# Two per-head totals as split fp32r matmuls, the request-state reads moved to the opening of a pair, and a reordered start, in a hybrid RWKV-7 decoder layer

## The reference

```python
n = rmsnorm(x, norm1)
c_rw, c_att, c_gate = _split(n @ w_in, (RW_COLS, ATT_COLS, GATE_COLS))
# RWKV-7 branch, 16 heads of 64
kk = heads(k * k_k)
kk = kk * lax.rsqrt(jnp.maximum(jnp.sum(kk * kk, axis=-1, keepdims=True), 1e-24))   # squared keys, total per head
S = S * w_t + sa[..., None] * b_t + v_t[..., None] * k_t                            # state, token by token
y = (y - mean) * lax.rsqrt(var + GN_EPS) * lnx_w + lnx_b                            # mean and variance per head
bonus = jnp.sum(r_h * k_h * r_k, axis=-1, keepdims=True) * v_h                      # total per head
out = (y + bonus) * g
# sparse attention branch, then
h = x + (sig(g_rw) * (o_rw @ p_rw) + sig(g_att) * (o_att @ p_att)) @ w_o
h = h + conv_glu(rmsnorm(h, norm2))
```

## Time and profile before

| | us |
|---|---|
| median of 3 runs | 1778.01 |
| range of the runs | 1776.01 to 1780.81 |
| profiled execution | 1776.88 |
| its span | 1775.3 |

### The profile page before, as it was taken

One profiled execution on the slowest core, in us unless ns is written; L12 is line 12 of the kernel. 1 busy time (PEld: TensorE's weight loads), 2 busy tenths in 40 slices (PEclk: granted clock), 3 DMA queues, 4 the chain that ended last, 5 costly groups with the idle time before them and its releaser, 6 DMA issues.

```text
span 1775.3 us, 40657 instructions
## 1 busy us (share of the span) xinstructions
PE 1758.8 (99%) x16482; PEld 1708.2 (96%) x16482; DVE 1120.7 (63%) x2015; ACT 759.6 (43%) x1059; POOL 53.8 (3%) x103
## 2 busy tenths in 40 slices
PE   9999999999999999999999999999999999999997
PEld 9999899999999998999999999999999999999997
DVE  7764864667777777665566666666666665444443
ACT  6456444555555554333443333333333333333332
POOL 2500000000000000000000000000000000000000
PEclk9999999999999999999999999999999999999998
DMA  7644344433333332644454444444444444555553
GB/s 285 220 165 165 124 162 157 143 115 118 112 112 117 112 111 103 220 166 170 171 220 163 157 164 158 168 161 167 164 165 165 165 165 167 172 169 175 170 169 134
DMA packets 51697, 283.47 MB, mean 160 GB/s; under 512 B 7248, under 2 KB 11856, under 8 KB 25776
## 3 DMA queue, kind: packets, MB, share of 16 engines
q1 hardware_dynamic: 43488, 260.32, 41.9%
q10 hardware_dynamic: 3888, 12.59, 1.9%
q0 software_dynamic: 4256, 9.65, 1.8%
HBM read 274.26 MB, written 8.27 MB: 159 GB/s over the span
## 4 chain that ended last, share of the span: by engine, by line
PE 96%; DVE 3%; DMA 0%; ACT 0%; issue 0%; DVEq 0%; ACTq 0%
PE bank L621 30%; PE bank L623 28%; PE bank L622 28%; PE bank L945 1%; PE bank L985 1%; DVE w_lo L567 1%; DVE scores L1939 1%; PE bank L642 0%; PE bank L643 0%; PE bank L644 0%; DMA w_raw<-in_w_in 0%; PE bank L905 0%; DVE max L1906 0%; PE bank L852 0%; PE bank L800 0%; PE bank L817 0%
## 5 line engine op out<-in xcount | busy, mean ns | idle before, releaser
L621 PE MATMUL bank<-x_split,w_lo 128*128 128x288 f32 x2880 | 872.8, 303 | 2.8 <-DVE w_lo L567 2.1
L622 PE MATMUL bank<-x_split,w_hi 128*128 128x288 f32 x2880 | 849.6, 295 | 0.0
L623 PE MATMUL bank<-x_split,w_hi 128*128 128x288 f32 x2880 | 847.2, 294 | 0.0
L587 ACT ACTIVATE w_hi<-w_raw 128x2048 fp32r<-128x2048 f32 (+1 forms) x262 | 468.7, 1789 | 591.8 <-PE bank L623 579.1
L567 DVE TENSOR_TENSOR w_lo<-w_raw,w_hi 128x2048 fp32r<-128x2048 f32 (+1 forms) x238 | 503.8, 2117 | 283.2 <-ACT w_hi L587 282.9
L621 PEld LDWEIGHTS bank<-x_split,w_lo 128*128 128x128 f32 x2880 | 540.3, 188 | 18.0 <-issue 8.2
L622 PEld LDWEIGHTS bank<-x_split,w_hi 128*128 128x128 f32 x2880 | 541.0, 188 | 2.6 <-issue 1.5
L623 PEld LDWEIGHTS bank<-x_split,w_hi 128*128 128x128 f32 x2880 | 542.2, 188 | 0.0
L621 PE MATMUL bank<-act_split,w_lo 128*128 128x288 f32 x704 | 208.5, 296 | 0.0
L622 PE MATMUL bank<-act_split,w_hi 128*128 128x288 f32 x704 | 207.7, 295 | 0.0
L623 PE MATMUL bank<-act_split,w_hi 128*128 128x288 f32 x704 | 207.0, 294 | 0.0
(11 more groups left out here) (396 smaller groups left out, 1544.2 us busy)
## 6 DMA issues: line engine op xcount, KB each, us to landing
w_raw<-in_w_up SPq DMA_DIRECT2D x88, 1024.0 KB, 4.8
w_raw<-in_w_in SPq DMA_DIRECT2D x47, 1024.0 KB, 4.9
w_raw<-in_w_down SPq DMA_DIRECT2D x64, 704.0 KB, 4.1
w_raw<-in_w_gate SPq DMA_DIRECT2D x32, 1024.0 KB, 4.8
w_raw<-in_w_p SPq DMA_DIRECT2D x16, 1024.0 KB, 4.9
w_raw<-in_w_o SPq DMA_DIRECT2D x16, 1024.0 KB, 4.8
h<-in_x ACTq DMA_DIRECT2D x1, 2304.0 KB, 11.2
h_spill<-h ACTq DMA_DIRECT2D x1, 2304.0 KB, 9.3
```

Source lines behind the costliest of these rows:

```text
L587: actv(WHI[:, slot, 0:kt], WRAW[:, slot, 0:kt], ACT.Copy).then_inc(sem("w_hi"), 3 if isinstance(n, int) and n == 2 else 1)
L621: mm(out, wl, hi, start=first and k == ks[0], stop=False, skip_group_check=True)
L622: mm(out, w, lo, start=False, stop=False, skip_group_check=True)
L623: ins = mm(out, w, hi, start=False, stop=last and k == ks[-1], skip_group_check=True)
```

## The change

- `kk_sum` and `bonus_mm` take their operand in rounded part and remainder (`SQS`, `RKS`, fp32r) and a matrix of ones in fp32r (`HONES`), in two matmuls each. ACT squares the keys twice (fp32 and rounded), DVE subtracts (`kk_lo`); for the bonus DVE copies `RKR` into its rounded part and subtracts, each waiting for the one before. Mean and variance stay as they are.
- The 16 products with `SIN` go from behind the fourth inverse step to a pair's opening, between lines 912 and 916. The wait for `bonus` comes with them, and the transposed columns move within bank 4.
- The chunk map of the last chunk has its own tile `MT3`; DVE makes five additions for the maps in place of four.
- DVE's additions to `SIN` (`s_grown`) come ahead of the last chunk's state, not behind it.
- In the first quarter of the first unit the x tiles 0 and 1 are rounded ahead of the weights, and PE starts with the four products that need rounded weights alone.

The start, on PE, ACT and DVE:

```diff
+                        if s == 0 and u == 0:
+                            pe.wait_ge(sem("w_part_hi"), 1)
+                            for k in range(2):
+                                pe.wait_ge(sem("x_split"), k + 1)
+                                mm(out, WHI[:, 0, k], XN[:, 0, k], start=k == 0, stop=False, skip_group_check=True)
+                                mm(out, WHI[:, 0, k], XN[:, 1, k], start=False, stop=False, skip_group_check=True)
...
+                        if s == 0 and u == 0:
+                            for k in range(2):
+                                mm(out, WLO[:, 0, k], XN[:, 0, k], start=False, stop=False, skip_group_check=True)
-                        for k in range(4):
+                        for k in range(2 if s == 0 and u == 0 else 0, 4):
...
+            first_hi(0, 2, "x_in0")
             act.wait_ge(sem("w_first_in"), 16)
             first_weights(0, [0])
-            first_hi(0, 2, "x_in0")
...
+            dve.wait_ge(sem("norms_in"), 16)
+            first_lo(0, 2)
             first_weights(0, [0])
-            dve.wait_ge(sem("norms_in"), 16)
-            first_lo(0, 4)
+            first_lo(2, 4)
```

The totals, on PE, ACT and DVE:

```diff
+            def head_sum(bank, split):
+                mm(BK[bank][:, 0:N], HONES[:], split[:, 1, :], start=True, stop=False, skip_group_check=True)
+                return mm(BK[bank][:, 0:N], HONES[:], split[:, 0, :], start=False, stop=True, skip_group_check=True)
             def kk_sum(v):
-                pe.wait_ge(sem("kk_sq"), v)
-                mm(BK[3][:, 0:N], head_ones, SQK[:], start=True, stop=True).then_inc(sem("kk_sum"), 1)
+                pe.wait_ge(sem("kk_sq"), 2 * v)
+                head_sum(3, SQS).then_inc(sem("kk_sum"), 1)
...
-                mm(BK[4][:, 0:N], head_ones, RKR[:], start=True, stop=True).then_inc(sem("bonus_mm"), 1)
+                head_sum(4, RKS).then_inc(sem("bonus_mm"), 1)
...
-                actv(SQK[:], RKV[:, 1, :], ACT.Square, scale=PRM[:, PR_KK:PR_KK + 1]).then_inc(sem("kk_sq"), 1)
+                for dst in (SQK[:], SQS[:, 0, :]):
+                    ins = actv(dst, RKV[:, 1, :], ACT.Square, scale=PRM[:, PR_KK:PR_KK + 1])
+                ins.then_inc(sem("kk_sq"), 1)
...
+            def kk_lo(v):
+                dve.wait_ge(sem("kk_sq"), 2 * v - 1)
+                V.tensor_tensor(SQS[:, 1, :], SQK[:], SQS[:, 0, :].bitcast(F32), ALU.subtract).then_inc(sem("kk_sq"), 1)
...
-                V.scalar_tensor_tensor(RKR[:], RKV[:, 0, :], PRM[:, PR_RK:PR_RK + 1], KP[:], ALU.mult,
-                                       ALU.mult).then_inc(sem("rkr"), 1)
+                st.done(V.scalar_tensor_tensor(RKR[:], RKV[:, 0, :], PRM[:, PR_RK:PR_RK + 1], KP[:], ALU.mult, ALU.mult))
+                st.done(V.tensor_copy(RKS[:, 0, :], RKR[:]))
+                V.tensor_tensor(RKS[:, 1, :], RKR[:], RKS[:, 0, :].bitcast(F32), ALU.subtract).then_inc(sem("rkr"), 1)
...
+            st.done(V.tensor_copy(HONES[:], head_ones))
+            kk_lo(1)
             streamed(FILL_FIRST)
             kk_max(1)
```

The pair, on PE (between lines 912 and 916; the same products go at 971 to 975, the wait for `bonus` at 924) and on DVE (the additions to `SIN` go from behind the loop over the chunks into its last pass):

```diff
+                pe.wait_ge(sem("bonus"), v)
+                pe.wait_ge(sem("sin_in"), v * 16)
+                settle(pe)
+                for r in range(2):
+                    for g, q in enumerate(quads):
+                        for e, h in enumerate(halves):
+                            mm(BK[(4, 7)[e]][q, 256 + r * HD:256 + (r + 1) * HD], ARS[h, r].rearrange("p x n -> p (x n)"), SIN[h, 4 * r + g, :],
+                               start=True, stop=True)
...
-                    ins = grown(grow, 0, 1, MTB[h, 2, e * HD:(e + 1) * HD], ST[h, 2, :], e, 1)
+                    ins = grown(grow, 0, 1, MT3[h], ST[h, 2, :], e, 1)
...
+                    if c == 3:
+                        dve.wait_ge(sem("state_s_mm"), v)
...
                     dve.wait_ge(sem("state_mm"), v * 3 - 3 + c)
                     state(c)
...
+                if not last:
+                    kk_lo(it + 2)
                 dve.wait_ge(sem("y_mm"), v)
```

More of the change, by code:

```diff
@@ L191 @@
 ATT_STEPS = [("sample", 0), (0, 0), (0, 1), (1, 0), (1, 1), ("sample", 1)]
-PAIR_STEPS = 16
+PAIR_STEPS = 18
 TOKEN_TILES = (0, P, N - P)
@@ L390, in build @@
     LO = m("l_off", [P, 2, 2 * BL])
-    MTB = m("chunk_map", [P, NCH - 1, P])
+    HONES = m("head_ones_r", [P, P], F32R)
+    MTB = m("chunk_map", [P, NCH - 2, P])
+    MT3 = m("chunk_map_3", [P, CH])
     MLS = region(vv_at)("m_low_s", [NS, 2, NS])
@@ L398, in build @@
     RKR = m("r_k_rk", [P, N])
+    RKS = m("r_k_rk_split", [P, 2, N], F32R)
+    assert m.at <= inv_at + 3 * size_of([P, 4, CH])
+    SQS = region(r0)("squares_k_split", [P, 2, N], F32R)
     m = region(big)
@@ L631, in first_units @@
                     for u in range(FIRST):
+                        out = BK[first_bank(u)][:, 0:N]
+                        if s == 0 and u == 0:
[4 more added lines that the diff above has]
+                                mm(out, WHI[:, 0, k], XN[:, 1, k], start=False, stop=False, skip_group_check=True)
                         if s < 2 and u < 3:
@@ L635, in first_units @@
                             pe.wait_ge(sem("w_split"), s + 1)
-                        out = BK[first_bank(u)][:, 0:N]
-                        for k in range(4):
+                        if s == 0 and u == 0:
+                            for k in range(2):
+                                mm(out, WLO[:, 0, k], XN[:, 0, k], start=False, stop=False, skip_group_check=True)
+                        for k in range(2 if s == 0 and u == 0 else 0, 4):
                             t = 4 * s + k
@@ L912, in pair @@
                             mm(BK[5 + e][q, tt * P:tt * P + BL], BT[h, c0:c0 + BL], AR[h, 0, c0:c0 + BL], start=True, stop=True)
+                quads = [slice(g * BL, (g + 1) * BL) for g in range(4)]
+                pe.wait_ge(sem("bonus"), v)
[6 more added lines that the diff above has]
+                               start=True, stop=True)
                 for tt, par in chunks:
@@ L923, in pair @@
                 ins.then_inc(sem("b_mm"), 1)
-                pe.wait_ge(sem("bonus"), v)
-                settle(pe)
                 for tt, par in chunks:
@@ L935, in pair @@
                 settle(pe)
-                tr(BK[4][:, 288:416], BKV[:].rearrange("p x n -> p (x n)"), ident).then_inc(sem("k_mm"), 1)
+                tr(BK[4][:, 384:512], BKV[:].rearrange("p x n -> p (x n)"), ident).then_inc(sem("k_mm"), 1)
                 fill(5)
-                quads = [slice(g * BL, (g + 1) * BL) for g in range(4)]
                 def blockwise(bank, lhs, rhs, both=False):
@@ L964, in pair @@
                 blockwise(3, L2, T)
-                pe.wait_ge(sem("sin_in"), v * 16)
                 pe.wait_ge(sem("mats"), v)
@@ L970, in pair @@
                 ins.then_inc(sem("l2s_mm"), 1)
[L971 to L975, removed]
                 for tt in range(2):
@@ L1512, in pair @@
                 for rows in (slice(0, 2 * NS), slice(2 * NS, P)):
-                    actv(TOKS[rows, 0, :], BK[4][0:2 * NS, 288:416], ACT.Copy)
-                actv(TOKS[NS:2 * NS, 1, :], BK[4][P - NS:P, 288:416], ACT.Copy).then_inc(sem("toks_sb"), 1)
+                    actv(TOKS[rows, 0, :], BK[4][0:2 * NS, 384:512], ACT.Copy)
+                actv(TOKS[NS:2 * NS, 1, :], BK[4][P - NS:P, 384:512], ACT.Copy).then_inc(sem("toks_sb"), 1)
                 if not last:
@@ L2230, in pair @@
                 state(0)
[L2231 to L2236, removed]
+                for c, src in ((1, BK[7][:, P:P + CH]), (2, BK[6][:, P + CH:2 * P])):
+                    for e, h in enumerate(halves):
+                        V.tensor_tensor(MTB[h, c - 1, e * HD:(e + 1) * HD], src[h], eye_ch[h], ALU.add)
+                V.tensor_tensor(MT3[:], BK[7][:, P + CH:2 * P], eye_ch, ALU.add).then_inc(sem("map"), 1)
                 rv = AR[:, 1, :].rearrange("p (c f) -> p c f", f=CH)
@@ L2247, in pair @@
                         mix_prev(it + 1, 0)
+                    if c == 3:
+                        dve.wait_ge(sem("state_s_mm"), v)
+                        for r in range(2):
+                            half = SIN[:, 4 * r:4 * r + 4, :]
+                            ins = V.tensor_tensor(half, half, BK[(5, 2)[r]][:, 0:256].rearrange("p (b f) -> p b f", f=HD), ALU.add)
+                        ins.then_inc(sem("s_grown"), 1)
                     dve.wait_ge(sem("state_mm"), v * 3 - 3 + c)
                     state(c)
[L2250 to L2254, removed]
+                if not last:
+                    kk_lo(it + 2)
                 dve.wait_ge(sem("y_mm"), v)
```

## The result

| | before | after |
|---|---|---|
| median of the runs, us | 1776.39 (20 runs) | 1780.88 (20 runs) |
| range of the runs, us | 1774.76 to 1780.81 | 1779.27 to 1783.40 |
| profiled execution, us | 1776.88 | 1781.10 |
| its span, us | 1775.3 | 1779.5 |

After to before: 1.0022, 95% interval 1.0016 to 1.0029. The changed kernel is 4.5 us slower, less than the 0.3% that the prediction set as its bound for a difference. It forecast +4.4 us. (The 1778.01 from which it counted was the median of three runs. With more of them it is 1776.39, so the predicted 1782.4 lies 1.5 us above the 1780.88.)

A forecast was written before the change was run, and what follows sets the result against it. PE, busy 99% of the span, bounds the kernel, with hidden waits for DVE. Terms 1.0 + 2.0 + 1.4 + 0 = +4.4 us give 1781.3 profiled, 1782.4 median; range 1776.5 to 1787, the forecast's own 1779.5 to 1785.

The forecast's parts named there:

- request-state reads: Products with SIN moved to a pair's opening: 0.25 us later up to position 16, in eight pairs, +2.0 us (1.8 to 3.0).
- totals in the pairs: Each fp32r total saves PE 0.21 us, but longer DVE work delays position 48: +0.14 a pair, seven pairs, +1.0 us.
- preparation: First pair's preparation: keys' total waits for ACT's second square, later DVE chain stalls PE near 353 us: +1.4 us (1.0 to 1.6).
- opening: Start of the kernel's first unit: second unit's weights still bound PE, clock could go either way: 0 (-0.9 to +0.65 us).
- The wait at position 16: Start of a pair's second unit: PE already waits a hidden 0.17 us for DVE's quarters, in all eight pairs.
- 0.38 - 0.16 = 0.22: Cost in us of the moved reads behind their own tile form: their 0.38 less 0.16 for a change of array tile.
- Rival 2: Moved reads cost 0.38 us each as before, split operations take upper ends: +7.3 us, 1785.3, slower by 0.4%; chance 0.30.
- Position 48: Later unit start in a pair: DVE's quarters, 0.88 us later, hold PE there to 0.35 us later than before.
- Rival 3: Preparation alone better than worked out, no wait at 353 us, pairs as forecast: +3.4 us, 1781.4; chance 0.10.
- The two possibilities that the prediction weighed: PE's clock in the opening: stays up, -0.9 us, or falls for 3.1 us later, inside work, +0.65 us.
- Costed at nothing: s_grown, kk_lo in the loop, ACT's second square and MT3 fall into idle time or behind cover: 0 us.
- Rival 1: PE's instruction sum alone decides, no late units at positions 16 and 48: -5.6 us, 1772.4; chance 0.10.

The follow-up runs named there:

- prep_fp32: Changed kernel, but the first pair's preparation takes its two totals in fp32 as the kernel before does: 1779.61 us.
- before_early: Kernel before, with DVE's first two split quarters for position 16 ahead of the inverse's first step, the other two ahead of its last: 1774.17 us.
- settle_first: Changed kernel with the waits for bonus and loaded states and the settling instruction ahead of the opening's first products, not right before the reads: 1779.93 us, single run.
- reads_back: Changed kernel with the reads of the states put back where the kernel before has them: 1777.35 us.
- k_late: Changed kernel with all four split quarters for position 48 ahead of DVE's mixed-keys step, instead of two ahead and two behind: 1778.39 us.
- best: Changed kernel with early split quarters at position 16, all four quarters ahead of the mixed keys at position 48, fp32 totals in first-pair preparation: 1771.47 us.

## Why the prediction was right, step by step

The forecast's mechanism held, and the sum, +4.4, came out at +4.5 in the medians and +4.2 between the two profiled executions. That is better than its terms, by luck: two were off by about 1 us each, in opposite directions.

| term | predicted | measured | by |
|---|---|---|---|
| request-state reads | 8 x 0.25 = +2.0 | 8 x 0.39 = +3.1 | first transposes to mean; undone, 3.3 us in the run |
| totals in the pairs | 7 x 0.14 = +1.0 | 7 x 0.02 = +0.1 | mean to the next pair |
| preparation | +1.4 | +1.35 | prep_fp32 and the two profiles |
| opening | 0 | -0.5 in one profile each | within the scatter below |

- **The wait at position 16** was read rightly from a distance of 0.30 us, and before_early shows that it was a wait. The rule that the first matmul of a waiting unit ends 0.52 us after DVE's quarter held there (507.56 to 508.08); at position 48 it is 0.46 (487.53 to 487.99).
- **The reads: the mis-sized term.** The step that failed is "0.38 - 0.16 = 0.22". It took the difference between lines 980 and 985 for the price of a change of array tile, and subtracted it. Behind their own tile form the reads add 0.45 us, and settle_first shows that the waiting and settling instructions have no part in it. The step behind it held: the reads' shift of the opening goes through DVE to position 16, and the gap that they leave at the old place is taken up by that wait. The wait grew by 0.43, near the 0.45, and the pair by 0.39. Rival 2's 0.38 a read was the better number for this term.
- **The drain rule.** The Trainium skill ("TensorEngine Tiling (Array Packing)", Key Properties) says that a change of tiling mode drains the array. Here the reads behind their own mode took 0.45 us and behind another 0.39 (in reads_back, 507.12 to 507.51), and with no wait behind them the pair was 0.04 us shorter at the place with the switch. By that rule alone the move would have saved time; it saved none that these runs can show. What a drain costs by itself no run here isolates.
- **Position 48.** The stall came where and as forecast, 0.46 us where 0.56 was implied (0.35 and the 0.21 by which PE comes earlier). DVE's chain grew by 0.83, not 0.88, mostly because the subtraction moved what is behind it by 0.37 and not 0.41; and the unit's first matmul follows by 0.46, not 0.52. These two make 0.11 of the 0.12 us between +0.14 and +0.02. The copy took the 0.31 us that the prediction chose; the subtraction beside it took 0.46. That agrees with what the Trainium skill says ("VectorE: DVE Perf Modes", Mode 2×_2P) of a copy against an operation of two tensors, also for an fp32r output, which the trace before could not show. The two totals' savings, 0.42, are what paid for the 0.46: k_late sets them free (-0.44 a pair).
- **The preparation** behaved as worked out: a first stall for the keys' total (0.59 us shown as idle, 0.86 by the distance of the ends) and a second one at 354 us (0.92). Less the 0.42 that the two totals save they make 1.36, the net that the prediction read off at the second stall. Rival 3 had the wait at 353 not coming, and is out. The reciprocal started 1.58 us later and not 2.1, since everything ahead of it ran 0.5 us early in this profile.
- **The opening.** In the changed kernel's profile PE starts its first products at 7.23 us, idles ahead of the second quarter's weights as forecast, and the granted clock does not fall, unlike in the earlier trace rows. The two stretches of the earlier trace rows in the profile after, then in reads_back with one more stretch (the same opening code), then in before_early (the opening of before) and in settle_first (the new opening):

```profile
9.70:11.00 1.30, 0.61 (x4) 0.61 (x5) 1.30 (x3) 1.30 (x4) 0.00 (x0) 1.00 1.00 422
11.00:12.80 1.80, 1.80 (x16) 1.80 (x15) 1.80 (x5) 1.76 (x5) 0.00 (x0) 1.00 1.03 395
```

```profile
9.70:11.00 1.30, 0.00 (x0) 0.00 (x0) 0.66 (x2) 1.30 (x3) 0.00 (x0) 1.00 1.01 429
11.00:12.80 1.80, 1.71 (x9) 1.71 (x10) 1.80 (x5) 1.80 (x5) 0.00 (x0) 0.71 0.95 393
12.80:14.60 1.80, 1.80 (x10) 1.80 (x9) 1.80 (x5) 1.80 (x5) 0.00 (x0) 0.50 0.68 176
```

```profile
9.70:11.00 1.30, 0.85 (x6) 0.62 (x5) 0.99 (x2) 1.30 (x4) 0.00 (x0) 1.00 1.01 429
11.00:12.80 1.80, 1.80 (x15) 1.80 (x15) 1.80 (x5) 1.80 (x6) 0.00 (x0) 1.00 0.95 393
```

```profile
9.70:11.00 1.30, 0.00 (x0) 0.00 (x0) 0.68 (x2) 1.30 (x3) 0.00 (x0) 1.00 1.00 422
11.00:12.80 1.80, 1.73 (x13) 1.73 (x14) 1.80 (x5) 1.80 (x5) 0.00 (x0) 1.00 0.97 398
```

  The clock fell to 0.50 (1.2 GHz) once with the new opening, after PE had stood idle through the stretch ahead, and stayed at 1.00 in one run of the old. In settle_first PE stood idle through the same stretch (1.60 us, 1.54 in reads_back) and the clock stayed at 1.00. So in these profiles neither the opening nor the length of that idle time tells whether the clock falls: it differs between executions. The two possibilities that the prediction weighed both occur. At the beginning of the prologue's last stall the eight profiles with the new opening stand between 224.4 and 226.4 us (mean 225.4), the two with the old at 225.0 and 225.5. The opening is worth 0 within about 1 us; nothing finer can be said.
- **Costed at nothing**: `s_grown`, `kk_lo` in the loop, `MT3` and ACT's second square brought no new wait of PE in a pair. DVE waits 1.10 us for the mean, 1.14 before.
- **The last pair and what follows** were not in the sum: +0.77 from the last pair's start, of which position 16 has its 0.4 and a longer pause (the last section) most of the rest, and -0.36 behind the pairs. That last stretch takes 952.4 us in four of the ten profiles, 952.7 in one and 953.1 in five, in no order that follows an edit.

Rival 1, PE's own sum alone, is out: the sum was indeed lower, and the time rose. Where its condition (no late unit at positions 16 and 48) was made true, in best, the time fell below the kernel before as it said, by 5.1 us where it had 5.6. But beside the saving of the totals this came from the old wait at 16 and the last pair's pause, not from a saved switch of tile or a better opening.

## What to carry to other kernels

On a busy engine read the distances of the ends, not the list of idle times: 0.17 us hidden in each pair decided that a shorter instruction sum would wait instead of gaining. When work moves, ask which other engine is released behind it, and carry the shift through that engine to the next place where its result is late; here this alone cost 3 us, and an earlier place for four quarters on DVE gave it back. And an edit that shortens PE by lengthening DVE should be made together with the order of DVE's steps: the same totals were worth +0.1 us with the quarters split around the longer step and -3 us with all of them ahead of it.

## What had not been expected of the hardware

- 32 matmuls of 64 columns in 64x32 tiles added 0.45 us behind products of the same tile form and 0.39 behind another. Staying in one tile form showed no saving.
- PE paused for 0.4 to 1.4 us where the trace shows neither a wait nor another engine ("issue"). In the profiles of before, after and four of the experiments the pause lies in the last pair, ahead of the third unit's first tile (0.71 us of idle time before, 0.95 after; by the distance of the ends 0.87 and 1.22 us are lost); reads_back has one more of 1.36 us in the first pair. In all four kernels with the early quarters it is absent, and 0.9 to 1.2 us of their gain is this. The DMA queue that carries instructions gives a lead. First PE's row behind the pause in the profile after, then that queue in the DMA view of 697.7 to 698.7 us (packets, MB, share):

```profile
700.14 0.40 PE L626 MATMUL bank<-x_split,w_lo 128*128 128x288 f32 x1 [0.95 <-issue]
```

```profile
q8 instruction: 1, 0.02, 5.5%
```

  This packet of 16 KB goes from 697.77 to 698.65 us. In all seven pauses such a packet starts 2.2 to 2.6 us before PE goes on and ends 1.4 to 1.6 us before. In the last pair of the six kernels with the pause it starts 24.1 to 25.1 us after the first transposes, in the four without it 19.9 to 20.1. So PE probably waits there for its next instructions. No run varied this, and why the early quarters bring the packet forward stays open.
